# Order of a bank's release, of k's second half, of the last pass's end and of the second layer's products in a fused encoder block

## The reference

```python
for l in range(DEPTH):                      # DEPTH 1, SEQ 1024, D_MODEL 1024, D_FF 4096
    xn = rms_norm(x, norm_mix_g[l])
    z = xn @ w_in[l]                        # columns B | C | h | q | k | v, 512 each
    y_conv = short_gated_conv(gb, gc, hh, conv_w[l], conv_b[l])       # width 3, per channel
    y_attn = chunk_band_attention(q, k, v, q_norm_g[l], k_norm_g[l], rel_bias[l])
    # 8 heads of 64; q and k rms-normalised per head; a chunk of 64 sees 9 chunks; bias by distance
    y_mix = concat(group_rms_norm(y_conv), group_rms_norm(y_attn))
    x = x + y_mix @ w_out[l]
    xn = rms_norm(x, norm_mlp_g[l])
    hid = square(relu(xn @ w_mlp_in[l]))
    x = x + hid @ w_mlp_out[l]
return x
```

## Time and profile before

| | us |
|---|---|
| median of three executions | 1160.19 |
| the profiled execution | 1159.96 |
| its span, first to last instruction | 1158.2 |
| TensorE busy in it | 1109.5 |
| VectorE, GpSimd, ScalarE busy | 724.5, 616.2, 539.7 |

### The profile page before, as it was taken

The page is one execution under the profiler, slowest core; times in us unless marked ns, Lnnn a source line. Parts: engine busy times, 40 slices in busy tenths (PEclk is TensorE's granted clock), DMA queues, the critical chain, the costliest instruction groups (busy, mean ns, idle before and its releaser), DMA issues.

```text
span 1158.2 us, 14651 instructions
## 1 busy us (share of the span) xinstructions
PE 1109.5 (96%) x5272; PEld 919.2 (79%) x5272; DVE 724.5 (63%) x899; ACT 539.7 (47%) x885; POOL 616.2 (53%) x339
## 2 busy tenths in 40 slices
PE   5989999998999989999999999999979999999998
PEld 4778877887887777887888888888868888888887
DVE  7667757766775777535342535343566677776788
ACT  6654554555465445224545454545543343243330
POOL 4122130321213022056877778787779698796992
PEclk9999999999999999999999999999989999999999
DMA  8310110111110423020464444445577536436324
GB/s 253 90 42 20 57 55 0 54 38 36 36 38 20 159 78 146 37 91 19 132 209 158 148 155 145 155 146 157 211 255 253 173 97 207 139 116 217 108 75 163
DMA packets 98511, 135.79 MB, mean 117 GB/s; under 512 B 8072, under 2 KB 52112, under 8 KB 98456
## 3 DMA queue, kind: packets, MB, share of 16 engines
q1 hardware_dynamic: 95104, 131.13, 33.9%
q10 hardware_dynamic: 3352, 3.94, 1.1%
HBM read 97.27 MB, written 39.34 MB: 118 GB/s over the span
## 4 chain that ended last, share of the span: by engine, by line
PE 84%; DVE 7%; ACT 4%; issue 3%; POOL 1%; DMA 1%; ACTq 0%; SPq 0%; DVEq 0%; POOLq 0%
PE PJ L1505 17%; PE PJ L1758 9%; PE SC L1758 9%; PE OS L1758 7%; PE PJ L1795 7%; PE PT L1795 6%; PE SC L1795 6%; PE OS L1795 6%; PE PJ L1583 5%; PE OS L1565 2%; PE PT L1552 2%; PE SC L1541 1%; PE SC L1542 1%; DVE sql L1024 1%; PE OS L1518 1%
## 5 line engine op out<-in xcount | busy, mean ns | idle before, releaser
L1505 PE MATMUL PJ<-actT,wsl 128*128 128x512 f32 (+1 forms) x1176 | 299.1, 396 | 1.8 <-ACT sqh L668 1.8
L1505 PEld LDWEIGHTS PJ<-actT,wsl 128*128 128x128 f32 x1176 | 209.8, 190 | 41.0 <-issue 3.5
L610 POOL TENSOR_TENSOR ring<-b,ring 128x1024 fp32r<-128x1024 f32 x48 | 137.8, 2878 | 38.5 <-ACT ring L952 38.0
L1412 DVE TENSOR_TENSOR ring<-hraw,ring 128x1024 fp32r<-128x1024 f32 x56 | 150.2, 2717 | 3.8 <-ACT ring L947 3.8
L504 POOL CAST wsl<-raw 128x1024 fp32r<-128x1024 f32 x24 | 26.0, 1084 | 219.4 <-PE PJ L1505 183.4
L947 ACT ACTIVATE ring<-hraw 128x1024 fp32r<-128x1024 f32 x56 | 59.2, 1058 | 135.1 <-PE OS L1795 63.6
L1758 PE MATMUL OS<-actT,w1a 128*128 128x512 f32 x384 | 93.6, 391 | 0.8 <-ACT p1s L888 0.8
L727 ACT ACTIVATE prob<-prob,negm 128x640 f32<-128x640 f32 (+4 forms) x64 | 44.5, 695 | 102.9 <-DVE negm L1111 102.8
L1795 PE MATMUL PJ<-ring 128*128 128x512 f32 x336 | 83.1, 398 | 6.0 <-POOL ring L610 4.4
L1758 PEld LDWEIGHTS OS<-actT,w1a 128*128 128x128 f32 x384 | 71.6, 188 | 15.6 <-issue 1.2
L1583 PE MATMUL PJ<-wo,actT 128*128 128x512 f32 x336 | 80.2, 393 | 3.0 <-POOL wo L520 1.6
(11 more groups left out here) (195 smaller groups left out, 2200.5 us busy)
## 6 DMA issues: line engine op xcount, KB each, us to landing
hraw<-hidd SPq DMA_DIRECT2D x56, 512.0 KB, 3.7
w1r<-in_w_mlp_in SPq DMA_DIRECT2D x16, 1024.0 KB, 6.4
hidd<-hs SPq DMA_DIRECT2D x64, 256.0 KB, 2.0
b<-in_w_mlp_out SPq DMA_DIRECT2D x16, 1024.0 KB, 6.8
raw<-in_w_in SPq DMA_DIRECT2D x24, 512.0 KB, 3.7
hidd<-h SPq DMA_DIRECT2D x48, 256.0 KB, 2.3
xin<-in_x SPq DMA_DIRECT2D x8, 512.0 KB, 8.6
woraw<-in_w_out SPq DMA_DIRECT2D x8, 512.0 KB, 7.9
```

The lines of the kernel that those rows point to most:

```text
L610: nc.gpsimd.tensor_tensor(duo(n)[1][LO], W2_SRC[name][:, 2 * d:2 * d + 2], duo(n)[1][HI].bitcast(F32), ALU.subtract).then_inc(s["wl2_done" ...
L1412: vec.tensor_tensor(duo(n)[0][LO], hraw[:, n % HRING], duo(n)[0][HI].bitcast(F32), ALU.subtract).then_inc(s["hl2_done"], 1)
L1505: last = mm(PJ[:, g % 2, cols], wsl[:, w % NSLOT, a, k], actT[:, b, k, c], start=(r == 0), stop=(r == 3 * KD - 1))
```

## The change

- Prologue: `x_lo(7)` moves behind `inverse(0, 0)` and `qk_scale(0, 0)`.
- Passes: `take(it, 3)` moves ahead of `deviation(it, 2)`; `qk_scale(it, 3)` from 5b to 5a; `qk_lo(it, 3)` from 6b to 6a; the scores of units 8 and 9 each wait for their own head's part of k.
- Last pass: `ym_lo(1)` moves from 15a to 14b, its `squares_lo` from 15a to 15b, `wo_hi(3)` ahead of `deviation(it, 5)`.
- Second layer: the products are ordered P1, P3, P2, P6, P7, P5, P4. Sum 0 goes to a tile of its own, t1 (in the place of first-layer tiles, with waits for their last readers), and P5 reads t1. Sum 2 is made at P7, sum 3 at P5. b22 is loaded two duos earlier than before, together with b12. All four accumulators are loaded at once, ahead of hidden block 5. `drain` waits for them at product 1.
- End: the folds and the stores of the outputs are put in another order.

```diff
-W2_ORDER = ("P1", "P6", "P2", "P5", "P7", "P3", "P4")
+W2_ORDER = ("P1", "P3", "P2", "P6", "P7", "P5", "P4")
...
+        t1 = nc.alloc_sbuf_tensor_at("t1", [P, 4, HALF], F32, offset=RB)
...
-        W2_SRC = {"P1": b11, "P6": t2, "P2": b21, "P5": b11, "P7": b12, "P3": b22, "P4": b21}
+        W2_SRC = {"P1": b11, "P6": t2, "P2": b21, "P5": t1, "P7": b12, "P3": b22, "P4": b21}
...
-            load_acc(0)
+            for j in range(4):
+                load_acc(j)
             load_hid(5)
...
-                if n < 9:
-                    load_acc(n - 5)
                 b, at = (n - 3) // 14, (n - 3) % 14
-                for tile, f, a, duo_, back, sem in ((b11, 0, 0, 7, 0, "b11_in"), (b12, 0, 1, 9, 0, "b12_in"),
-                                                    (b22, 1, 1, 11, 0, "b22_in"), (b21, 1, 0, 13, 0, "b21_in")):
+                for tile, f, a, duo_, back, sem in ((b11, 0, 0, 7, 0, "b11_in"), (b22, 1, 1, 9, 0, "b22_in"),
+                                                    (b12, 0, 1, 9, 0, "b12_in"), (b21, 1, 0, 13, 0, "b21_in")):
...
             sp.wait_ge(s["fin_done"], 5)
+            sp.dma_start(out_t[:, 0:4, half(1)], acc[:, 1]).then_inc(s["out_written"], 16)
+            sp.wait_ge(s["fin_done"], 6)
             sp.dma_start(out_t[:, 4:8, half(1)], acc[:, 3]).then_inc(s["out_written"], 16)
-            sp.wait_ge(s["dr_done"], 2 * (NPROD2 - 1))
-            sp.dma_start(out_t[:, 0:4, half(1)], acc[:, 1]).then_inc(s["out_written"], 16)
...
-                    nc.gpsimd.tensor_tensor(b11[:, c], b12[:, c], b11[:, c], ALU.subtract).then_inc(s["ts_done"], 1)
+                    if b == 0 and d == 0:
+                        pool.wait_ge(s["c21_done"], NF)
+                    if b == 0 and d == 1:
+                        pool.wait_ge(s["c22_done"], NF)
+                        pool.wait_ge(s["hs_done"], 4 * (NF - 2) + 3)
+                        pool.wait_ge(sp_out["h11_0"], 16 * (NF // 2))
+                    pool.wait_ge(s["b11_in"], 16 * (b + 1))
+                    nc.gpsimd.tensor_tensor(t1[:, c], b12[:, c], b11[:, c], ALU.subtract).then_inc(s["ts_done"], 1)
...
-                    nc.gpsimd.tensor_tensor(t2[:, c], b22[:, c], b11[:, c], ALU.subtract).then_inc(s["ts_done"], 1)
+                    nc.gpsimd.tensor_tensor(t2[:, c], b22[:, c], t1[:, c], ALU.subtract).then_inc(s["ts_done"], 1)
...
+                if name == "P7":
+                    w2_sum(b, 2, d)
                 if name == "P5":
-                    w2_sum(b, 2, d)
-                if name == "P3":
                     w2_sum(b, 3, d)
...
                     if u == 2:
+                        take(it, 3)
                         deviation(it, 2)
-                        take(it, 3)
...
                 else:
+                    wo_hi(3)
                     deviation(it, 5)
 
                     act.wait_ge(s["pv_done"], NPAIR * UNITS)
-                    wo_hi(3)
...
                 if at == "5a":
                     inverse(it, 3, 0)
                     inverse(it, 3, 1)
+                    qk_scale(it, 3)
                 if at == "5b":
-                    qk_scale(it, 3)
                     qk_lo(it, 2)
-                if at == "6b":
+                if at == "6a":
                     qk_lo(it, 3)
...
-                if at == "15a" and last:
+                if at == "14b" and last:
                     ym_lo(1)
+                if at == "15b" and last:
                     squares_lo(it, 5)
...
-            for t in range(4, NT):
+            for t in range(4, NT - 1):
                 x_lo(t)
...
             qk_scale(0, 0)
+            x_lo(NT - 1)
             inverse(0, 1, extra=1)
...
-                if name == "P2" and q < 7:
+                if q == 1:
                     dve.wait_ge(s["acc_in"], 64)
...
                     fold(2, 4, 0)
+                    fold(1, 4, 0)
+                if q == NPROD2 - 3:
+                    dve.wait_ge(s["dr_done"], 2 * q)
                     fold(2, 5, 1)
-                if q == NPROD2 - 3:
-                    fold(1, 4, 2)
                 if q == NPROD2 - 2:
                     dve.wait_ge(s["dr_done"], 2 * q)
-                    fold(3, 4, 3)
-                    fold(3, 6, 4)
+                    fold(3, 4, 0)
                 drain(q)
+            dve.wait_ge(s["dr_done"], 2 * (NPROD2 - 1))
+            fold(1, 6, 2)
+            fold(3, 6, 4)
...
-                if u == 8:
-                    pe.wait_ge(s["qklo_done"], it * 6 + 6)
-                    pe.wait_ge(s["kdup_done"], it * 4 + 4)
+                if u in (8, 9):
+                    pe.wait_ge(s["qklo_done"], it * 6 + (u - 3))
+                    pe.wait_ge(s["kdup_done"], it * 4 + (u - 5))
```

## The result

The changed kernel takes 1163.32 us (median of 20 executions, 1162.0 to 1165.15) beside 1160.18 for the kernel before: the ratio is 1.0025, 95% interval 1.0016 to 1.0033. The forecast was 1159.1, a gain of 0.1%. The time rose instead, and the forecast is 4.2 us too low. The profiled execution has a span of 1161.4 us against 1158.2.

What follows compares the result with a forecast made beforehand. TensorE was taken to bound the kernel. 1159.96 - 1.5 (prologue) - 10.7 (k) - 0 (bank) - 2.7 (last pass) + 13.8 (second layer) = 1158.9, set to 1159.1 us against the median; range 1155 to 1163, chance 0.50.

Steps and rivals of the forecast that it cites:

- What bounds: Whole kernel: TensorE, busy 1109.5 of 1158.2 us, sets the end.
- the prologue: Prologue: the first inverse no longer waits behind tile 7's split; gain 1.5 us, bounds 1.0 and 1.9.
- the 49 us: Whole kernel: time TensorE stands still or runs at the lower clock, all that can be won or lost.
- k's second half: Four passes: unit 8's score no longer waits for kL; gain 10.7 us, bounds 9.5 and 10.8.
- The bank's release: Passes: removes a 0.46 us wait, but TensorE then waits longer for the squares' split; gain 0, bounds 0 and 1.8.
- End of the last pass: Last pass: earlier split and weight copy remove waits, some given back; gain 2.7 us, bounds 3.4 and a 0.5 loss.
- The second layer: Second layer: bunched sums make GpSimd late at P7 and P5; waits 22.6 against 8.8 us before, cost 13.8.
- rival 3: Second layer: close waits, deciding above 2.45 us, drop the clock to 1.2 GHz, 2.4 us each; two give 1164; chance 0.18.
- The port: Second layer: VectorE's two-input SBUF splits and GpSimd lock each other out; if shared by halves, block loss near 0.
- rival 1: Second layer: GpSimd keeps up wholly, so 18.8 us of new waits fall away: 1140 us; chance 0.12.
- The end: Kernel's end: last drain and 256 KB store unchanged, moved foldings fit; 0, bounds 0.3 us either way.
- terms of -15 and +14: Gains of 1.5, 10.7 and 2.7 us ahead of the second layer, against the second layer's cost of 13.8 us.

Runs made afterwards that it cites:

- relback: The changed kernel with ScalarE's take(it, 3) put back behind deviation(it, 2): 1163.06 us.
- ymlate: The changed kernel with the last pass's split of tile 1, ym_lo(1), moved behind the o_sum of units 12 and 13: 1161.72 us.
- early2: The kernel before with only the change's parts ahead of the second layer, and tile 1's split behind the o_sum: 1142.25 us.
- lean: The changed kernel with VectorE's low part of the hidden tiles cut to 64 of 512 columns from the second block on: 1150.94 us.
- early: The kernel before with only the change's parts ahead of the second layer, whose order, sums, loads, folds and stores stay: 1145.39 us.

## Why the prediction was wrong

- **What bounds, and the prologue.** Right but for the end, which TensorE doesn't set (below), and for the 49 us: the page counts the time at the lower clock as busy, so it comes on top of them. Gain 1.84 us at the first score (49.52 instead of 51.36), where 1.5 was predicted; at the second sum of squares 1.75 of it is there (41.46 instead of 43.21).
- **k's second half.** Right: no wait on kL is left. The period fell by 2.63 us, over four passes 10.5 of the predicted 10.7.
- **The bank's release.** Right: 0, by moving a wait (run `relback`); L1530 waits 0.9 us, where 0.7 was named.
- **End of the last pass.** The mechanisms were right, the term was 1.2 us too large: 1.5 instead of 2.7. The step that failed is the sentence that put tile 1's split at 425.8 to 427.0: it looked at what GpSimd does then, and not at what is queued behind it on VectorE. `o_sum` is, and `prob_v` waits for it. Without that (run `ymlate`, 1.3 us; `early2`, from 404.63 to 452.65 48.0 us against 50.8 before) the stage gives 2.8. (The profiled executions of before, the changed kernel and `early2` all have a fall of the clock in it, so they can be compared.)
- **The second layer.** The mechanism and the late duos were as predicted: the second of P7 and both of P5, in every block, and in block 0 the second of P6 by 2.2 us, with GpSimd's low part of duo 5 ending at 851.66 (865.5 was reckoned in the times of the kernel before, where duo 2 starts 13.8 us later: 851.7). Predicted from duo 2 on: 8.9 + 2.5 + 2.5 + 7 = 20.9 us; measured 8.7 + 2.7 + 2.6 + 8.2 = 22.2. Before: 7.1, measured 7.1. The 1.3 us too little lie in the last block, where rival 3 came true once (1.7 us). That block 0 was met within 0.2 us is partly luck: its first P7 duo was to be late by 1.5 us for GpSimd and was late by 1.7 for the clock, and with the same code there the other runs lose 9.2 to 10.6.
- **The port.** Right, and stronger than written: rival 1 stood on GpSimd's idle time, and `lean` shows that with short splits it would keep up.
- **Rival 3, the clock.** Its condition, waits above the 2.45 us that had left the clock at full, was wrong. It fell behind waits of 1.99 to 2.05 us. The trace of the kernel before held such a case and the prediction didn't see it: behind the wait of 1.99 us at 417.19 the granted clock is 0.50 from 419 to 421. One of the two falls of this stage is in the 8.7 of block 0 (the next duo would otherwise have waited), and the other was free, because the end didn't hang on TensorE.
- **The end.** This is the step with the largest error: 0 was predicted, with 0.3 to either side, and 1.9 us were lost (3.6, counted without the free fall of the clock; then the last block has 6.5 of the predicted 7). I counted the foldings' time, 6.8 us, against TensorE's 10.9, and forgot three things that the rows held: that the folding ahead of the drains would be held up by GpSimd, that a folding behind the drains must end before 1 MB can leave, and that this store lies in one queue ahead of the last one. A store "unchanged" in code wasn't unchanged in time. The step that failed is the path: the last drain and its 256 KB don't end the kernel, in either version. The first of the last 3 MB does, 10.05 us before the end, and one of the two foldings put behind the last but one drain is what that store waits for. It left 3.2 us later than before (1151.35, 1148.12), and the span is 3.2 us longer.

The errors add up: 0.2 + 1.2 + 1.3 + 1.9, less 0.3 in the prologue, are the 4.3 us between the predicted span (1157.1) and 1161.4. With a forecast of 0.1% and terms of -15 and +14, an error of a tenth in one of them turns the sign. Rival 3's time was 1164, at 0.18.

## What to carry to other kernels

A change of order that wins in one stage and loses in another should be taken apart before it is judged: here one half is worth 14 to 16 us and the other costs 17 to 18. On an engine that runs close to its consumer, work must be counted at its stretched price and spread over the stretch, and all of what is queued behind a moved instruction has to be listed, not only what it meets. Look at the end of a kernel as a chain of its own (last product, drain, folding, store, queue), since it can take a loss, or hide one, that TensorE doesn't show.

## What the hardware showed that I had not expected

The same wait is followed by a fall of the granted clock in one execution and not in another. TensorE's row behind the same wait in the last block, of the changed kernel:

```profile
1137.98 4.58 PE L1807 MATMUL PT<-ring 128*128 128x512 f32 x12 [2.04 <-POOL ring L617]
```

and of run `ymlate`:

```profile
1135.07 2.97 PE L1807 MATMUL PT<-ring 128*128 128x512 f32 x12 [2.04 <-POOL ring L617]
```

In both, the two duos before it waited 1.7 and 2.0 us. The same holds in the last pass, at 405 us: behind a wait of 1.99 us the clock was 0.50 in the changed kernel and in `early2` (and, at 419 us, in the kernel before), and 1.00 in `early` and `ymlate`; it makes 1.1 us between executions. The four waits of 2.3 to 2.45 us in the passes of the kernel before were not followed by one. The runs don't settle what decides it, so a price of 1.1 to 1.8 us with a chance below one belongs to each wait of 2 us.
